# A hybrid attention layer on one core: memory rows turned un-normed, one-instruction squares, first loads and turns in another order

## The reference

```
def rmsnorm(x, g):
    xf = x.astype(jnp.float32)
    y = xf * lax.rsqrt(jnp.mean(xf * xf, axis=-1, keepdims=True) + EPS)
    return (y * g.astype(jnp.float32)).astype(x.dtype)

def memory_cross_attention(q, mem_h, w_mem_kv, q_gain, k_gain):
    kv = mem_h @ w_mem_kv
    k, v = jnp.split(kv, 2, axis=-1)
    k = rmsnorm(k.reshape(B, M, MEM_HEADS, MEM_HEAD_DIM), k_gain)
    ...

h = rmsnorm(x, ln_gain[l]);  proj = h @ w_in[l]
mem_h = rmsnorm(mem, mem_ln_gain[l])
```

## Time and profile before

| | us |
|---|---|
| median of 3 runs | 2826.0 |
| lowest and highest | 2823.24, 2828.24 |
| the profiled execution, its own time | 2824.71 |
| its span, first to last instruction | 2822.9 |
| PE busy | 2756.2 |
| memory stage, from the start to the first matmul of the first group | 90.96 |

### The profile page before, as it was taken

How to read it: one execution, slowest core, us unless ns; L and a number is a source line. 1 busy time by engine, 2 the same in 40 slices (tenths; PEclk the granted TensorE clock), 3 DMA queues, 4 the chain that set the end, 5 groups by cost and what they waited for, 6 DMA issues and landing times.

```text
span 2822.9 us, 37249 instructions
## 1 busy us (share of the span) xinstructions
PE 2756.2 (98%) x12859; PEld 2269.6 (80%) x12859; DVE 1390.3 (49%) x2419; ACT 1018.9 (36%) x2125; POOL 1286.5 (46%) x552
## 2 busy tenths in 40 slices
PE   6999999999999999999999999999999999999999
PEld 5888887888888888788888888788888888878887
DVE  5345575333525556614534557542534455753335
ACT  6333434333323343424332343433332234343333
POOL 4545543444444543344445454344444454434444
PEclk9999999999999999999999999999999999999999
DMA  6333333335533332334443333233453333333354
GB/s 213 113 93 102 113 101 98 109 127 168 167 96 99 97 120 94 102 101 152 164 143 98 106 97 112 90 112 112 154 175 119 90 98 112 101 100 107 126 170 142
DMA packets 215830, 337.94 MB, mean 120 GB/s; under 512 B 17702, under 2 KB 77172, under 8 KB 212852
## 3 DMA queue, kind: packets, MB, share of 16 engines
q1 hardware_dynamic: 194644, 283.49, 32.5%
q10 hardware_dynamic: 21024, 52.44, 5.4%
HBM read 293.13 MB, written 17.56 MB: 110 GB/s over the span
## 4 chain that ended last, share of the span: by engine, by line
issue 57%; POOL 40%; PE 1%; SPq 1%; POOLq 1%; DMA 0%; DVE 0%; ACT 0%; ACTq 0%
POOL w_lo L428 36%; POOL q_scale L434 2%; POOL early L442 1%; SPq L356 1%; POOLq L427 0%; DMA raw<-in_w_mem_kv 0%; POOL x_scale L434 0%; PE acc L1140 0%; PE acc L1142 0%; PE acc L1141 0%; POOL k_scale L434 0%; ACT w_hi L496 0%; SPq L358 0%; PE ps_t L1193 0%; POOLq L473 0%
## 5 line engine op out<-in xcount | busy, mean ns | idle before, releaser
L428 POOL TENSOR_TENSOR w_lo<-raw,w_hi 128x1024 fp32r<-128x1024 f32 x482 | 1176.8, 2441 | 1503.5 <-ACT w_hi L496 1503.5
L496 ACT ACTIVATE w_hi<-raw 128x1024 fp32r<-128x1024 f32 x482 | 509.7, 1057 | 1331.7 <-PE acc L1142 1308.9
L1140 PE MATMUL acc<-h_hi,w_hi 128*128 128x512 f32 x1792 | 706.4, 394 | 3.6 <-DVE ungated L1031 3.5
L1141 PE MATMUL acc<-h_lo,w_hi 128*128 128x512 f32 x1792 | 699.8, 391 | 0.0
L1142 PE MATMUL acc<-h_hi,w_lo 128*128 128x512 f32 x1792 | 699.4, 390 | 0.0
L1140 PE MATMUL acc<-w_hi,mix_hi 128*128 128x512 f32 x1088 | 428.1, 393 | 16.9 <-DVE stage L1125 9.4
L1141 PE MATMUL acc<-w_lo,mix_hi 128*128 128x512 f32 x1088 | 424.8, 390 | 0.0
L1142 PE MATMUL acc<-w_hi,mix_lo 128*128 128x512 f32 x1088 | 424.8, 390 | 0.0
L1140 PEld LDWEIGHTS acc<-h_hi,w_hi 128*128 128x128 f32 x1792 | 337.5, 188 | 81.3 <-DVE ungated L1031 4.2
L1142 PEld LDWEIGHTS acc<-h_hi,w_lo 128*128 128x128 f32 x1792 | 337.5, 188 | 71.1
L1141 PEld LDWEIGHTS acc<-h_lo,w_hi 128*128 128x128 f32 x1792 | 337.4, 188 | 68.3
(11 more groups left out here) (150 smaller groups left out, 2254.5 us busy)
## 6 DMA issues: line engine op xcount, KB each, us to landing
raw<-in_w_in SPq DMA_DIRECT2D x336, 512.0 KB, 3.7
raw<-in_w_out SPq DMA_DIRECT2D x130, 512.0 KB, 3.6
probs_t<-blocks_t SPq DMA_DIRECT2D x384, 64.0 KB, 2.1
xt<-in_x ACTq DMA_DIRECT2D x16, 1024.0 KB, 6.7
stage<-in_x ACTq DMA_DIRECT2D x64, 256.0 KB, 5.5
out<-stage ACTq DMA_DIRECT2D x64, 256.0 KB, 3.0
raw<-in_w_mem_kv SPq DMA_DIRECT2D x16, 512.0 KB, 7.8
ungated<-in_x SPq DMA_DIRECT2D x2, 1024.0 KB, 13.7
```

What stands on the lines that cost most here:

```text
L428: nc.gpsimd.tensor_tensor(w_lo[:, slot_mod % 2, :], raw[:, slot_mod, :], w_hi[:, slot_mod % 2, :].bitcast(F32), ALU.subtract).then_inc(lo_ ...
L496: nc.scalar.activation(w_hi[:, slot_mod % 2, :], raw[:, slot_mod, :], ACT.Copy).then_inc(hi_ready, 1)
L1140: nc.tensor.matmul(dst, st[0], mv[0], start=first, stop=False)
L1141: nc.tensor.matmul(dst, st[0], mv[1], start=False, stop=False)
```

## The change

- **Memory rows.** They are turned as they come from DRAM, without their factor. The factor (now kept in `mem_scale`, one column for each tile) is applied by ACT where it moves keys and values out of PSUM. `mem_turn` waits for the load alone. The last four of the eight quads are turned behind slots 0 and 1 (`MEM_TURNS`) and split on ACT at indices 0 and 2 (`MEM_HIGH_AT`).
- **Squares.** `x_square` is one instruction of 128 x 2048 into SBUF (`dump`, or `flipped` in the output passes) instead of four of 128 x 512 into PSUM, and the sum over four columns on DVE is gone. All six squares of the memory stage lie behind `high` at indices 1, 3, 4, 5, 6 and 8 (`FIRST_SQ_AT`), their powers on POOL behind `low` at 2, 4, 5, 6, 7 and 9 (`FIRST_ITEM_AT`).
- **Loads.** SP begins with weight slots 0 and 1; six of the seven small vector loads are behind them. The four x tiles are behind slots 3, 5, 7 and 9 (`X_LOAD_AFTER`), `one_hot`, `rel_bias` and `sinks` behind slot 4, and the write of `bias_rows` is now ahead of slot 8's load instead of behind it.
- **Turns of x.** None before slot 9; then 2, 2, 2, 2, 3, 3, 2 (`FIRST_TURNS`). The power for the memory keys is taken at index 9 instead of 8.

The diff, without the lines that only declare or drop semaphores and small tiles:

```diff
@@ -94,7 +94,14 @@
-FIRST_TURNS = [[]] * 5 + [[0], [1], [2], [3, 4], [5, 6], [7, 8], [9, 10], [11, 12], [13, 14], [15], []]
+FIRST_TURNS = [[]] * 9 + [[0, 1], [2, 3], [4, 5], [6, 7], [8, 9, 10], [11, 12, 13], [14, 15]]
+MEM_TURNS = {0: (4, 5), 1: (6, 7)}
+MEM_HIGH_AT = {0: (4, 5), 2: (6, 7)}
+FIRST_SQ_AT = {1: 0, 3: 1, 4: 2, 5: 3, 6: 4, 8: 5}
+FIRST_ITEM_AT = {2: 0, 4: 1, 5: 2, 6: 3, 7: 4, 9: 5}
+X_LOAD_AFTER = {3: 0, 5: 1, 7: 2, 9: 3}
+CONSTS_AFTER = 4
+K_RSQRT_AT = 9
 K_TURN_MEM = 12
@@ -147,7 +154,9 @@
         h_hi = sb("h_hi", [P, KT, TOK], F32R)
+        dump_at = -(-nc.sbuf_base // 32) * 32
         h_lo = sb("h_lo", [P, KT, TOK], F32R)
+        dump = nc.alloc_sbuf_tensor_at("dump", [P, KT, P], F32, offset=dump_at + (KT - 4) * TOK * 4)
@@ -342,35 +351,38 @@
-            vec(MEM_GAIN, KT, mem_ln_gain[0].rearrange("(k p) -> k p", p=P))
-            vec(GAIN, KT, ln_gain[0].rearrange("(k p) -> k p", p=P))
...
-            for s in range(4):
-                weights(s, s, True, w_mem_kv[256 * s:256 * s + 256, 0:512])
-            for tile in range(TT):
-                sp.dma_start(first_rows(2 + tile), x[P * tile:P * tile + P, :].rearrange(
-                    "p (k c) -> p k c", c=P)).then_inc(first_in[2 + tile], 16)
-            sp.dma_start(probs_t[0:BUCKETS, 0, :, :].rearrange("p a b -> p (a b)")[:, 0:REL],
-                         one_hot).then_inc(c_dma, 16)
-            sp.dma_start(rel_tab[:, :], rel_bias).then_inc(c_dma, 16)
-            for half in range(2):
-                sp.dma_start(sink[64 * half:64 * half + 64, :],
-                             bass.AP(sinks.tensor, half, [[0, 64], [2, 8]]),
-                             allow_slow_non_contiguous=True).then_inc(c_dma, 16)
-            for s in range(4, MEM_SLOTS):
-                weights(s % 4, s, False, w_mem_kv[256 * (s % 8):256 * (s % 8) + 256,
+            def mem_weights(s):
+                weights(s % 4, s, s < 4, w_mem_kv[256 * (s % 8):256 * (s % 8) + 256,
                                                   512 * (s // 8):512 * (s // 8) + 512])
+
+            for s in range(MEM_SLOTS):
                 if s == BIAS_AT + 5:
                     sp.wait_ge(bias_sb, 1)
                     sp.dma_start(bias_rows[:, :, 0:REL],
                                  probs[0:16, 0, 0:REL].unsqueeze(1).broadcast_to([16, CHUNK, REL])
                                  ).then_inc(bias_out, 16)
+                mem_weights(s)
+                if s == 1:
+                    vec(GAIN, KT, ln_gain[0].rearrange("(k p) -> k p", p=P))
...
+                if s in X_LOAD_AFTER:
+                    tile = X_LOAD_AFTER[s]
+                    sp.dma_start(first_rows(2 + tile), x[P * tile:P * tile + P, :].rearrange(
+                        "p (k c) -> p k c", c=P)).then_inc(first_in[2 + tile], 16)
+                if s == CONSTS_AFTER:
+                    sp.dma_start(probs_t[0:BUCKETS, 0, :, :].rearrange("p a b -> p (a b)")[:, 0:REL],
+                                 one_hot).then_inc(c_dma, 16)
+                    sp.dma_start(rel_tab[:, :], rel_bias).then_inc(c_dma, 16)
...
             sp.wait_ge(bias_out, 16)
@@ -442,17 +454,17 @@
             def x_item(tile):
-                rsqrt(x_scale[:, :], x_mean[:, 1:2], 1, x_meaned, tile + 1, x_rstd)
-
-            x_item(0)
-            x_item(1)
+                first = isinstance(tile, int) and tile < 2
+                rsqrt(mem_scale[:, tile:tile + 1] if first else x_scale[:, :], x_mean[:, :], 1,
+                      x_meaned, tile + 1, x_rstd)
+
             low(0, 0)
             low(1, 1)
             for s in range(MEM_SLOTS):
                 low((s + 2) % 4, s + 2)
-                if s < TT:
-                    x_item(2 + s)
-                if s == SB_SLOTS:
+                if s in FIRST_ITEM_AT:
+                    x_item(FIRST_ITEM_AT[s])
+                if s == K_RSQRT_AT:
                     rsqrt(k_scale[:, :], k_mean[:, :], 8, k_meaned, 1, k_rstd)
@@ -501,15 +515,11 @@
-            def x_square(tile, rows):
+            def x_square(tile, rows, squares):
                 if not isinstance(tile, int) or tile:
-                    act.wait_ge(x_summed, tile)
-                for q in range(4):
-                    if not isinstance(tile, int) or tile or q:
-                        act.wait_ge(x_squares, tile * 4 + q)
-                    nc.scalar.activation(ps_z[:, :].rearrange("p (k c) -> p k c", c=P),
-                                         rows[:, 4 * q:4 * q + 4, :], ACT.Square,
-                                         accum_out=x_sq[:, q:q + 1]).then_inc(x_squares, 1)
+                    act.wait_ge(x_meaned, tile)
+                nc.scalar.activation(squares, rows, ACT.Square,
+                                     accum_out=x_sq[:, :]).then_inc(x_squares, 1)
@@ -636,33 +646,34 @@
-            act.wait_ge(first_in[0], 16)
-            x_square(0, first_rows(0))
             act.wait_ge(vecs_turned, 1)
             nc.scalar.activation(vecs[:, :], ps_o[:, 0:VECS], ACT.Copy).then_inc(vecs_ready, 1)
-            act.wait_ge(first_in[1], 16)
-            x_square(1, first_rows(1))
+            high(0, 0, True)
             act.wait_ge(vecs_ready, 1)
-            high(0, 0, True)
-            for quad in range(8):
-                mem_high(quad)
-                if quad == 1:
-                    high(1, 1, True)
+            mem_high(0)
+            mem_high(1)
+            high(1, 1, True)
+            mem_high(2)
+            mem_high(3)
             for s in range(MEM_SLOTS):
                 if s == SB_SLOTS - 1:
                     for m in range(2):
                         act.wait_ge(slot_used, SB_SLOTS) if m else act.wait_ge(dense_done, 1)
-                        nc.scalar.activation(stage[:, 2 + m, :], acc[m][:, :],
-                                             ACT.Copy).then_inc(bank_free[m], 1)
+                        act.wait_ge(x_rstd, m + 1)
+                        nc.scalar.activation(stage[:, 2 + m, :], acc[m][:, :], ACT.Copy,
+                                             scale=mem_scale[:, m:m + 1]).then_inc(bank_free[m], 1)
                 if s == MEM_SLOTS - 1:
                     for m in range(2):
                         act.wait_ge(slot_used, MEM_SLOTS) if m else act.wait_ge(dense_done, 2)
-                        nc.scalar.activation(mem_v[:, m, :], acc[m][:, :],
-                                             ACT.Copy).then_inc(bank_free[m], 1)
+                        nc.scalar.activation(mem_v[:, m, :], acc[m][:, :], ACT.Copy,
+                                             scale=mem_scale[:, m:m + 1]).then_inc(bank_free[m], 1)
                 high((s + 2) % 4, s + 2)
-                if s < TT:
-                    act.wait_ge(first_in[2 + s], 16)
-                    x_square(2 + s, first_rows(2 + s))
+                for quad in MEM_HIGH_AT.get(s, ()):
+                    mem_high(quad)
+                if s in FIRST_SQ_AT:
+                    tile = FIRST_SQ_AT[s]
+                    act.wait_ge(first_in[tile], 16)
+                    x_square(tile, first_rows(tile), dump[:, :, :])
                 if s == BIAS_AT:
@@ -708,7 +719,8 @@
                             act.wait_ge(x_in, (g * TT + n) * 16 + 16)
-                            x_square(tile, xt[:, :].rearrange("p (k c) -> p k c", c=P))
+                            act.wait_ge(x_free, 8 + KT + 4 * (g * TT + n))
+                            x_square(tile, xt[:, :], flipped[:, :, :].rearrange("p a b -> p (a b)"))
                         if s in X_HIGH_AT:
@@ -730,14 +742,14 @@
-            def x_norm(tile, rows):
-                dve.wait_ge(x_squares, tile * 4 + 4)
-                nc.vector.tensor_reduce(x_mean[:, 0:1], x_sq[:, :], AX.X,
-                                        ALU.add).then_inc(x_summed, 1)
-                dve.wait_ge(x_summed, tile + 1)
-                nc.vector.tensor_scalar(x_mean[:, 1:2], x_mean[:, 0:1], 1.0 / D, EPS,
+            def x_means(tile):
+                dve.wait_ge(x_squares, tile + 1)
+                nc.vector.tensor_scalar(x_mean[:, :], x_sq[:, :], 1.0 / D, EPS,
                                         ALU.mult, ALU.add).then_inc(x_meaned, 1)
                 dve.wait_ge(x_rstd, tile + 1)
+
+            def x_norm(tile, rows):
+                x_means(tile)
                 nc.vector.tensor_scalar(rows, rows, x_scale[:, 0:1], None,
@@ -1041,6 +1051,8 @@
                 mem_low(quad)
+            for tile in range(2):
+                x_means(tile)
             for tile in range(2, 2 + TT):
@@ -1053,13 +1065,10 @@
             dve.wait_ge(c_dve, 6)
-            before_keys = FIRST_TURNS[SB_SLOTS - 1][-1] + 1
-            for k in range(before_keys):
-                first_low(k)
             mem_keys = stage[:, 2:4, :].rearrange("p m c -> p (m c)")
             key_means(mem_keys, xt[:, 0:1024], M_HEAD, 1, mem_raw)
-            before_scale = FIRST_TURNS[SB_SLOTS + 1][-1] + 1
-            for k in range(before_keys, before_scale):
```

(12 more changed lines are left out.)

26 lines of the change are left out of this document (16 added, 10 removed).

## The result

Over ten runs each, the changed kernel took 2835.34 us (2834.07 to 2836.81) and the kernel before 2825.83. The ratio is 1.0033, with a 95% interval of 1.0023 to 1.0043: slower, and by more than the 0.2% that a measurement can tell. The forecast was 2833.

A forecast was written before the change was run, and what follows sets the result against it. PE, busy 98% of the span, bounds the kernel. Memory-stage gains, waits and clock losses start the first group at 98.2 instead of 90.96, 7.2 later; 7 us on the 2826.0 median gives 2833, own range 2829 to 2836, overall 2825 to 2838.

The forecast's parts named there:

- The start: Memory stage, start: slot 0 starts at 16.7 us, 7.5 earlier than before.
- Slots 1 to 7: Memory stage: slot 7 ends at 46 us against 59.4 before, so PE is 13 us ahead.
- Slot 8's load: SP's queue: held behind the small loads and the bias_rows write, it lands at 50.3 us (50.0 to 51.9).
- the load isn't held: Rival, SP's queue: the bias_rows write doesn't hold slot 8's load, landing before about 43; 2823 us, chance 0.12.
- The wait ahead of slot 8: Memory stage: PE idles from 46 to 54.2 us, for slot 8's load and then ACT's work.
- The clock: Memory stage: the lower clock behind each of PE's two long waits costs 2.8 us.
- no clock loss: Rival, memory stage: the clock isn't lost at the two waits, or returns at once; 2827.6 us, chance 0.12.
- The last tile's factor: Behind slot 9: PE waits 5.7 us for the last x tile's scaling, so turns start at 68.4.
- The rest: From the first turn of x to the first group: 29.8 us, so the first group starts at 98.2.
- third turns: Where three turns follow each other, the third waits for the first's low part: 1.1 us in two places, 2.2.
- More clock losses where turns stand thick: Rival, behind slots 13 and 14: one or two more clock losses of 2.8 us; 2836 to 2839, chance 0.13.
- Output passes: Rival: PE's 11.7 us of waits for DVE's add come back, 2821.5 us, chance 0.05; the forecast took 0.

The follow-up runs named there:

- e1: The changed kernel with the write of bias_rows behind slot 8's load on SP instead of ahead of it; 2831.48 us, ratio 1.0019.
- e3: The changed kernel with POOL's power for the last x tile ahead of slot 11's low instead of behind it; 2833.44 us, ratio 1.0023.
- e4: The changed kernel with unused matmuls filling PE's two long waits (40 behind slot 7, 24 behind slot 9); 2830.77 us, ratio 1.0016.
- e5: The changed kernel with one_hot, rel_bias and the sinks loads on ACT's queue instead of SP's; 2829.45 us, ratio 1.0008.
- e6: The changed kernel with one_hot, rel_bias, sinks and the write of bias_rows all on ACT's queue; 2824.62 us, ratio 0.9989.
- e2: The changed kernel with the write of bias_rows issued on ACT's queue, behind ACT's copy of the values; 2831.26 us, ratio 1.0016.
- e10: The kernel before with one-instruction squares, and the small loads and write of bias_rows on ACT's queue; 2821.78 us, ratio 0.9984.
- e11: e6 with the last tile's square at index 7, its power at 8 and its load behind slot 8's; 2825.23 us, ratio 0.9994.
- e7: The kernel before with only the one-instruction squares, without DVE's sum; 2824.97 us, ratio 0.9989.

## Why the prediction was right

- **The start** (slot 0 at 16.7, from PE's first instruction at 11.5): 16.71. PE's first instruction came at 11.86, still for the small vector loads.
- **Slots 1 to 7** (13 us ahead at slot 7's end): 11 us. The loads landed later than I added up (x tiles at 36.7 and 44.6 instead of 34.5 and 40.6): the small loads took from 19.5 to 32.3, 12.8 us where I took 10.0. This is the term with the largest error, and it moved slot 8's load as well. Slot 0, for which I had charged 2 us of half pace, ran at full pace and ended at 19.8 instead of 21.5, but PE spent that waiting for `sinks`; in e1 it ran at half pace, and PE didn't wait.
- **Slot 8's load** (50.3, range to 51.9): 53.7, outside my range, and by e3's and e4's profiles 51.2 and 52.6 for the same queue, so it varies by over 2 us from run to run. That the sum came within 3.4 is in part luck: the tile ahead landed 4.0 late, the write landed 6.3 behind it and not 8.1 to 10.0, and the load 2.8 behind the write and not 1.3. The mechanism is shown by e1 (the write ahead of it), e5 (`sinks`) and e6 (both: 39.6). The rule in the prediction's sum, one queue served in order, is borne out, and the rival "the load isn't held" fell: it asked for a landing before 43, which needed both edits (e6; e1's 43.7 comes near). The Trainium skill, "DMA: Bandwidth & Descriptors", section on queues, rings and completion order, says that each engine takes a ring's descriptors in order and takes turns between the rows that have work. By that rule a write on another queue still takes a share, and e2 agrees: the load gained 4 us at most, not the write's whole 10. So does e10, where `sinks` on ACT's queue slowed the weight loads on SP's.
- **The wait ahead of slot 8** (idle from 46 to 54.2, 8.2): 9.18. PE restarts at 57.36, 3.2 later than forecast. ACT's part was as added up (1.06, 1.89 for the square where I took 2.1, and 0.6 for the first move).
- **The clock** (2.8 at each wait): the lower level reached to 60.7 behind slot 8's start and to 74.3 behind the first turn, half of 3.3 and of 4.1 us: 1.65 and 2.05. The mechanism was right and the two terms together 1.9 too high. I had not foreseen the third stretch, over slot 4, which by luck cost nothing. Before, the lower clock lay on 5.8 us of work behind the wait (43.95 to 49.8), here on 3.3 and 4.1: what counts is how much of it lies on work. The rival "no clock loss" fell. e4 took the lower clock away and got back 2 of the 3.7, since POOL is the next bound behind the first wait.
- **The last tile's factor** (5.7): 5.55. In e3 and e11, which reorder POOL and ACT, only 0.7 and 0.8 us of it came back.
- **The rest** (29.8 from the first turn to the first group): 30.28. The two third turns waited 1.79 each, and I had 1.1: 1.4 too low. ACT was not free for the first turn's split, since a `high` stands ahead of it there (87.84 to 88.80). The clock term gave 0.75 of that back (2.05 for 2.8).
- **More clock losses where turns stand thick** fell: the window from 88 to 98 shows 1.00, with two waits of 1.79 in it. Where a turn of x was slow (from 70.19), the clock was low anyway. In the first 17 us the quads of memory rows were slow too, at a granted clock that the profile gives as 1.00; but so were slot 0's matmuls in e1 (0.63 us, 0.39 at full clock), so the half pace that the prediction read off the quads at 20.47 says nothing of turns as such. The Trainium skill, "TensorE: Matmul & The Clock Gate", Part 4 on PE-mode transposes, has it that they don't count as PE being busy in the way matmuls do. No loss is to be seen here that would come of it; turns are only 0.87 us of each slot's 3.65, and 1.3 of each 6.05 behind slots 13 and 14, so this case can't refute the rule, only the price that I gave it.
- **Output passes**: no change in the 11.7, in the changed kernel and in e7.

The sum was 7.2 for the memory stage. It was 9.5 in the two profiles, and the medians differ by 9.5 (2835.34 less 2825.83); that these agree to the tenth is chance, as the profiled execution of the changed kernel was its slowest (2836.81) and that of the kernel before 1.1 below its median. Of the 2.3 that lack, slot 8's late start is 3.2 and the third turns 1.4, the clock gives 1.9 back, and small gaps another 0.4. The spans differ by 11.8: one more slow stretch in the first group (the row at 470) is 1.7 of it. Which of the groups have one differs from run to run (all four in the changed kernel and in e3, three in the kernel before and in e2 and e4), so it is no part of the change that I could show.

What stays open: whether x could be scaled early enough with a column of `x_sq` for each tile, so that squares need not wait for means. That wasn't tried. Nor was the un-normed start together with e10's spread turns.
